# One turn and one product a pair in the first attention: VectorE combines both heads' weights

## The chip, the cores and the metric

The program runs on one core of one Trainium2 chip. The metric is device time in microseconds (us) of one execution, the median of several. Five engines share a core's on-chip memory, and each works through its own list of instructions in order: TensorE (PE: matrix products and transposes), VectorE (DVE), ScalarE (ACT), GpSimd (POOL) and SyncE (SP, here the DMA queue). They meet through semaphores: an instruction waits until a counter has reached a value, and another instruction raises it.

## The reference

The program computes two small transformer stacks one after the other on 256 tokens of width 1024, in float32. The change touches the first attention of the first stack only, the differential attention, once in each of its 2 layers (DEPTH = 2, A_HEADS = 4):

```python
y_a = diff_attention(aq.reshape(b, s, A_HEADS, 2, HEAD_DIM),
                     ak.reshape(b, s, A_HEADS, 2, HEAD_DIM),
                     av.reshape(b, s, A_HEADS, 2 * HEAD_DIM),
                     lam, lam_init, a_subln[i]).reshape(b, s, A_WIDTH)
```

Each of its 4 heads is a pair: two sets of queries and keys of width 64 give two score matrices of 256 by 256 with a mask by chunks of 64. Each has its own softmax, and both are applied to the same values of width 128. The output is the first product minus lambda times the second. Since the values are shared, (P1 V) - lambda (P2 V) is the same as (P1 - lambda P2) V, up to rounding.

## The kernel before

Tokens lie on the 128 partitions, in two tiles (T = 2). Weights come from HBM in tiles of 512 rows by up to 512 columns (1 MB), into a ring of 4 raw buffers. ScalarE copies each raw tile to a rounded "high" part (`high_part`, L1248), VectorE subtracts to get the "low" part (`low_part`, L1665), and TensorE makes three products for each of 4 row blocks and 2 token tiles (L665 to L667), 24 for a tile. High and low parts have 3 buffers, so that they are made some tiles ahead (`ahead`, which calls `split_to`).

The order of the work is written out by hand, in one program for each engine; no planner changes it later. A stage is a function of the same name on each engine. The stage here is `pairs` with `use == "A"`. `plan_of` deals out a list of weight tiles (the projections that later stages need) so that TensorE has products while a softmax goes on: one tile before and one after the first turn, then for pairs 0 to 3 the shares of 1, 2, 1 and 2 tiles, and two tiles held for the end (`hold`). The first two tiles in the shares have 324 columns, the others 512. Beside the tiles, the table `beside` gives VectorE work for the third attention (its norms and rotations: L1905, L1910, L1916 and the index keys, L1688 to L1979), which it does at a fixed place in its order.

For a pair n the chain is as follows, with a number of pairs of 4 in each of the 2 layers, so 8 in all.

- TensorE turns queries and keys (`start_turn_qk`, L763), ScalarE copies them (`copy_qk`, L1394), TensorE makes the scores of both heads into banks 5 and 6 (`pair_scores`, L779).
- VectorE adds the mask and takes the row maximum (`mid`, L2103 to L2112), ScalarE takes the exponential and the row sum (L1429), and VectorE takes the reciprocal of the sums and multiplies the second head's by minus lambda (`take_probs`, L2120 and L2123).
- TensorE turns the unscaled weights of both heads, 6 blocks (`turn_probs`, L818), ScalarE copies them in one piece of 768 columns (L1435), TensorE multiplies both with the values into bank 7 (`values`, L832).
- VectorE reads bank 7, scales the two halves by their row factors and adds them (`finish`, L2140 and L2143).

TensorE's place for this is fixed: scores of the pair, the tiles of its share up to three quarters of the last, the turn of the weights, the turn of the next queries and keys, the last quarter, and the products with the values. Where a share has one tile, that tile comes whole before the turn. VectorE's place is: mask and maximum of pair n, `finish` of pair n-1, the low parts of the share's tiles, the reciprocal, the work beside the tiles. ScalarE makes the high parts ahead of the exponentials.

After pair 3 TensorE starts on the two held tiles, and half way through the first it turns the index keys, which VectorE has to have rotated by then (`index_roped`). The next stage is `sticks` (the second attention), which ScalarE enters when VectorE has done its last instruction of `pairs` (`dve_done`).

## Time and profile before

| | us |
|---|---|
| median of 3 executions | 3175.24 |
| lowest, highest | 3172.05, 3179.62 |
| the profiled execution, its own time | 3178.99 |
| its span | 3177.2 |
| TensorE busy in the span | 3043.9 (96%) |
| VectorE busy | 2293.4 (72%) |
| ScalarE busy | 1755.9 (55%) |

The span is what the profiler saw from the first to the last instruction, and the device time of the same execution is 1.8 us longer. The two stages that the change touches run at about 77 to 142 us and 588 to 653 us of the span. TensorE's busy time counts a product until the modelled end of its result, so successive products overlap; how long one takes of the engine's time is read from the distance of two starts.

### The profile page before, as it was taken

What the parts mean: (1) busy time and instruction counts of PE and PEld (TensorE: products, weight loads), DVE (VectorE), ACT (ScalarE), POOL (GpSimd) and SP (SyncE); (2) the same over time, 40 slices, a digit from 0 to 9 for tenths busy, and PEclk for the clock granted to TensorE, in tenths of its full rate; (3) what the DMA queues carried; (4) which work ended last, traced back from release to release, by engine and by line L of the source; (5) the groups of instructions that cost most, each with busy time, mean ns of one, the idle gap of its engine ahead of it and who ended that gap; (6) DMA issues with size and microseconds to landing.
All of it is one profiled execution on the core that took longest, in us unless ns stands there. A gap on an engine that the chain in (4) does not pass through costs nothing.

```text
span 3177.2 us, 37793 instructions
## 1 busy us (share of the span) xinstructions
PE 3043.9 (96%) x14818; PEld 2484.5 (78%) x14818; DVE 2293.4 (72%) x2365; ACT 1755.9 (55%) x1657; POOL 46.2 (1%) x28
## 2 busy tenths in 40 slices
PE   8999999999999899998998999979999999999998
PEld 6777887877888787777887877768878888888786
DVE  7887556887645655776446666767888888888888
ACT  4565445465445345463433454626777777777765
POOL 0000000100000000000000000000000000000000
PEclk9999999999999999999999999989999999999999
DMA  7434555434555554335554543339999999999997
GB/s 247 146 128 157 185 183 174 161 120 142 179 186 179 170 168 160 119 133 185 185 172 159 181 163 110 129 97 344 347 359 338 349 361 338 353 361 343 359 342 260
DMA packets 351088, 697.24 MB, mean 219 GB/s; under 512 B 12224, under 2 KB 17216, under 8 KB 350784
## 3 DMA queue, kind: packets, MB, share of 16 engines
q1 hardware_dynamic: 347024, 687.75, 63.0%
q10 hardware_dynamic: 3888, 7.07, 0.7%
q8 instruction: 119, 1.95, 0.2%
q14 instruction: 57, 0.47, 0.0%
HBM read 693.73 MB, written 1.05 MB: 219 GB/s over the span
## 4 chain that ended last, share of the span: by engine, by line
PE 73%; DVE 11%; DMA 5%; ACT 4%; DVEq 3%; issue 3%; PEld 0%; POOL 0%; ACTq 0%; PEldq 0%
PE banks L665 22%; PE banks L667 21%; PE banks L666 21%; DVE weights_low L1665 5%; DMA weights_raw<-in_moe_w_down_dram 3%; ACT weights_high L1248 3%; DMA weights_raw<-in_moe_w_up_dram 1%; PE banks L1159 1%; PE banks L702 1%; DMA weights_raw<-in_moe_w_gate_dram 1%; PE banks L779 1%; PE banks L763 1%; PE banks L788 1%; PE banks L1097 1%; PE banks L1208 1%
## 5 line engine op out<-in xcount | busy, mean ns | idle before, releaser
L1665 DVE TENSOR_TENSOR weights_low<-weights_raw,weights_high 128x2048 fp32r<-128x2048 f32 (+1 forms) x658 | 1489.8, 2269 | 511.1 <-ACT weights_high L1248 506.3
L1248 ACT ACTIVATE weights_high<-weights_raw 128x2048 fp32r<-128x2048 f32 (+1 forms) x658 | 1247.4, 1899 | 551.0 <-PE banks L667 432.6
L665 PE MATMUL banks<-weights_high,h_transposed_high 128*128 128x512 f32 x2784 | 1107.5, 398 | 20.9 <-DVE weights_low L1665 11.0
L667 PE MATMUL banks<-weights_high,h_transposed_low 128*128 128x512 f32 x2784 | 1084.7, 390 | 0.0
L666 PE MATMUL banks<-weights_low,h_transposed_high 128*128 128x512 f32 x2784 | 1083.8, 389 | 0.0
L665 PEld LDWEIGHTS banks<-weights_high,h_transposed_high 128*128 128x128 f32 x2784 | 526.1, 189 | 145.5 <-DVE weights_low L1665 16.2
L667 PEld LDWEIGHTS banks<-weights_high,h_transposed_low 128*128 128x128 f32 x2784 | 525.7, 189 | 110.5
L666 PEld LDWEIGHTS banks<-weights_low,h_transposed_high 128*128 128x128 f32 x2784 | 526.7, 189 | 101.7 <-issue 1.0
L665 PE MATMUL banks<-weights_high,y_transposed_high 128*128 128x512 f32 x1000 | 396.8, 397 | 6.5 <-DVE y_transposed_low L2525 2.4
L667 PE MATMUL banks<-weights_high,y_transposed_low 128*128 128x512 f32 x1000 | 390.0, 390 | 0.0
L666 PE MATMUL banks<-weights_low,y_transposed_high 128*128 128x512 f32 x1000 | 389.5, 390 | 0.0
L665 PEld LDWEIGHTS banks<-weights_high,y_transposed_high 128*128 128x128 f32 x1000 | 187.7, 188 | 53.2 <-issue 7.1
L667 PEld LDWEIGHTS banks<-weights_high,y_transposed_low 128*128 128x128 f32 x1000 | 187.7, 188 | 40.0
L666 PEld LDWEIGHTS banks<-weights_low,y_transposed_high 128*128 128x128 f32 x1000 | 187.9, 188 | 36.9
L2560 POOL TENSOR_TENSOR rsqrt<-mean_squares,minus_half 128x2 f32<-128x2 f32 (+3 forms) x23 | 45.8, 1993 | 3124.1 <-DVE mean_squares L1677 1564.7
L1394 ACT ACTIVATE qk_transposed<-banks 128x512 f32<-128x512 f32 x68 | 38.6, 568 | 68.7 <-PE banks L763 64.4
L1367 ACT ACTIVATE projected<-banks 128x512 f32<-128x512 f32 x34 | 20.3, 596 | 97.2 <-PE banks L667 97.2
L1571 ACT ACTIVATE y_transposed_high<-banks 128x1024 fp32r<-128x1024 f32 (+1 forms) x22 | 22.2, 1007 | 87.4 <-PE banks L1097 87.4
L1429 ACT ACTIVATE scratch<-scratch,minus_row_max 128x256 f32<-128x256 f32 (+1 forms) x128 | 56.7, 444 | 24.7 <-DVEq L2112 24.4
L1304 ACT ACTIVATE h_transposed_high<-banks 128x512 fp32r<-128x512 f32 x32 | 17.9, 596 | 94.0 <-PE banks L702 94.0
L2397 DVE TENSOR_TENSOR y_transposed_low<-banks,y_transposed_high 128x1024 fp32r<-128x1024 f32 (+1 forms) x22 | 26.4, 1200 | 58.9 <-ACT y_transposed_high L1571 58.9
L702 PE MATMUL banks<-constants,x_residual 128*128 128x128 f32 x160 | 26.3, 319 | 39.7 <-DVE x_residual L2346 33.0
(326 smaller groups left out, 2184.5 us busy)
## 6 DMA issues: line engine op xcount, KB each, us to landing
weights_raw<-in_w_in_dram SPq DMA_DIRECT2D x152, 1024.0 KB, 5.0
weights_raw<-in_moe_w_gate_dram SPq DMA_DIRECT2D x114, 1024.0 KB, 6.6
weights_raw<-in_moe_w_up_dram SPq DMA_DIRECT2D x112, 1024.0 KB, 6.3
weights_raw<-in_moe_w_down_dram SPq DMA_DIRECT2D x112, 1024.0 KB, 6.5
weights_raw<-in_w_up_dram SPq DMA_DIRECT2D x32, 1024.0 KB, 5.4
weights_raw<-in_w_down_dram SPq DMA_DIRECT2D x32, 1024.0 KB, 5.0
weights_raw<-in_ffn_w_gate_dram SPq DMA_DIRECT2D x10, 1024.0 KB, 5.1
weights_raw<-in_ffn_w_up_dram SPq DMA_DIRECT2D x10, 1024.0 KB, 5.1
```

What stands on the lines that cost most here:

```text
L665: nc.tensor.matmul(out_of[t], lhs(0, k, t), high[:, k], start=begin, stop=False)
L666: nc.tensor.matmul(out_of[t], lhs(0, k, t), low[:, k], start=False, stop=False)
L667: mm = nc.tensor.matmul(out_of[t], lhs(1, k, t), high[:, k], start=False, stop=end)
L702: tr = nc.tensor.transpose(PS[:, t["banks"][b], at:at + P], buf[t["src"]][:, i, t["cols"][k]:t["cols"][k] + P], ident)
L763: tr = nc.tensor.transpose(PS[:, bank, i * P:(i + 1) * P], x[:, t, col:col + P], ident)
L779: mm = nc.tensor.matmul(PS[:, bank + h, cols], z[rows, q * P:(q + 1) * P], zk[rows, S:S + keys], start=True, stop=True)
L788: mm = nc.tensor.matmul(PS[h * HD:(h + 1) * HD, 7, col + cols.start:col + cols.stop], PR[:, kt, v0[h]:v0[h] + HD], weights[:, h, at:at + c ...
L1248: nc.scalar.activation(tile_view(WH, h % SPLIT, tile), tile_view(raw, h % RAW, tile), ACT.Copy).then_inc(high_ready, 1)
L1394: nc.scalar.activation(QKT[:, (n - 1) % 2, 0:cols], PS[:, bank, 0:cols], ACT.Copy).then_inc(qk_copied, 1)
L1429: nc.scalar.activation(probs, probs, ACT.Exp, bias=NMX[:, i:i + 1], accum_out=SUM[:, i:i + 1])
L1665: v.tensor_tensor(tile_view(WL, h % SPLIT, tile), tile_view(raw, h % RAW, tile), tile_view(WH, h % SPLIT, tile).bitcast(F32), ALU.subtract ...
L2560: nc.gpsimd.tensor_tensor(RSTD[:, 0:n], STAT[:, 0:n], MHALF[:, 0:n], ALU.pow).then_inc(rsqrt_ready, 1)
```

## The change

The second head's weights are scaled by its factor, the first head's are scaled and the second's added to them, by four VectorE instructions on the weights themselves, in place (`take_probs`). TensorE then turns 3 blocks and not 6 (`turn_combined`, into bank 7, whereas before they went to banks 5 and 6), ScalarE copies 384 columns and not 768, TensorE makes 3 products with the values and not 6 (`values_combined`, into bank 4), and `finish` is one copy.

The order changes on three engines. TensorE: the turn of the weights moves from three quarters of the last tile to its end, the next pair's scores come ahead of the products with the values, the share's last tile is always cut in quarters, and the turn of the next queries and keys, which writes the same bank 4, waits for `values_read`. ScalarE: the exponentials come ahead of the share's high parts, and the copy of queries and keys ahead of the copy of the turned weights. VectorE: `take_probs` always comes ahead of the share's low parts.

```diff
-                def turn_probs():
-                    pe.wait_ge(probs_ready, c.add("probs") + c.of("scaled"))
-                    for h in range(2):
-                        for i in range(3):
-                            tr = nc.tensor.transpose(PS[:, 5 + h, i * P:(i + 1) * P], SM[:, h, i * P:(i + 1) * P], ident)
+                def turn_combined():
+
+                    pe.wait_ge(probs_scaled, c.add("scaled"))
+                    wait_low(turned_in.get(7, 0))
+                    for i in range(3):
+                        tr = nc.tensor.transpose(PS[:, 7, i * P:(i + 1) * P], SM[:, 0, i * P:(i + 1) * P], ident)
                     tr.then_inc(probs_turned, 1)
...
+                def values_combined(n):
+
+                    _, _, (v0, _), _ = pair_cols(use, n)
+                    pe.wait_ge(probs_act, c.of("scaled"))
+                    pe.wait_ge(qk_copied, c.of("qk"))
                     for t in range(T):
-                        for h in range(2):
-                            for kt in range(t + 1):
-                                o = (2 * t + h) * vw
-                                mm = nc.tensor.matmul(PS[:, 7, o:o + vw], PT[:, h, (kt + t) * P:(kt + t + 1) * P],
-                                                      PR[:, kt, v0[h]:v0[h] + vw], start=kt == 0, stop=kt == t)
+                        for kt in range(t + 1):
+                            mm = nc.tensor.matmul(PS[:, 4, t * P:(t + 1) * P], PT[:, 0, (kt + t) * P:(kt + t + 1) * P],
+                                                  PR[:, kt, v0:v0 + P], start=kt == 0, stop=kt == t)
                     mm.then_inc(values_full, 1)
+                    c.add("values")
...
                 def pair_turn(n):
 
+                    if c.of("values"):
+                        pe.wait_ge(values_read, c.of("values"))
                     start_turn_qk(*pair_cols(use, n)[:2], bank=4 if use == "A" else 6, same_keys=use == "W" and n % 2 == 1)
...
                 if use == "A":
+                    pair_scores(5).then_inc(scores_full, 1)
                     for n in range(N):
-                        pair_scores(5).then_inc(scores_full, 1)
-                        late = shares[n][-1] if len(shares[n]) > 1 else None
-                        for p, i in shares[n]:
-                            if (p, i) != late:
-                                step(st, p, i)
-                        if late:
-                            for part in range(3):
-                                tile_step(*late, part, 4)
-                        turn_probs()
+                        for p, i in shares[n][:-1]:
+                            step(st, p, i)
+                        for part in range(3):
+                            tile_step(*shares[n][-1], part, 4)
                         if n + 1 < N:
                             pair_turn(n + 1)
-                        if late:
-                            tile_step(*late, 3, 4)
-                        values(n)
+                        tile_step(*shares[n][-1], 3, 4)
+                        turn_combined()
+                        if n + 1 < N:
+                            pair_scores(5).then_inc(scores_full, 1)
+                        values_combined(n)
...
                     act.drain().then_inc(probs_ready, 1)
                     if use == "A":
-                        act.wait_ge(probs_turned, c.add("turned_probs"))
-                        nc.scalar.activation(PT[:], PS[:, 5:7, 0:384], ACT.Copy).then_inc(probs_act, 1)
+                        for p, i in shares[n]:
+                            ahead(p, i)
+                            for what in beside_of(p, i):
+                                beside(p, what)
                         if n + 1 < N:
                             copy_qk(4)
+                        act.wait_ge(probs_turned, c.add("turned_probs"))
+                        nc.scalar.activation(PT[:, 0], PS[:, 7, 0:384], ACT.Copy).then_inc(probs_act, 1)
...
                         v.tensor_scalar(by_t(RS)[:, :, 1], by_t(RS)[:, :, 1], LAM[:, st["layer"], 1:2], None, ALU.mult)
                         dve.drain()
+                        one, two = (by_tile(SM[:, h]) for h in range(2))
+                        for t in range(T):
+                            v.tensor_scalar(two[t], two[t], RS[:, 2 * t + 1:2 * t + 2], None, ALU.mult)
+                        dve.drain()
+                        for t in range(T):
+                            i = v.scalar_tensor_tensor(out=one[t], in0=one[t], scalar=RS[:, 2 * t:2 * t + 1], in1=two[t],
+                                                       op0=ALU.mult, op1=ALU.add)
+                        i.then_inc(probs_scaled, 1)
...
-                        v.tensor_tensor(first, o[:, :, 0], by_t(RS)[:, :, 0].unsqueeze(2).broadcast_to([P, T, P]), ALU.mult)
-                        dve.drain()
-                        for t in range(T):
-                            i = v.scalar_tensor_tensor(out=PR[:, t, n * P:(n + 1) * P], in0=o[:, t, 1], scalar=RS[:, 2 * t + 1:2 * t + 2],
-                                                       in1=first[:, t], op0=ALU.mult, op1=ALU.add)
-                        i.then_inc(values_read, 1)
+                        v.tensor_copy(PR[:, :, n * P:(n + 1) * P], PS[:, 4, 0:S].rearrange("p (t d) -> p t d", t=T)).then_inc(values_read, 1)
...
+                    take_probs()
+                    for p, i in shares[n]:
+                        ahead(p, i)
```

The held tile's turn of the index keys also waits for `values_read` now, as it writes bank 4 too.

Two places show how the order moves. The first is TensorE around the last quarter of pair 1's second tile, before the change: L818 turns the weights (`scratch`), L763 turns the next queries and keys out of `projected`, L832 is the products with the values, L779 the scores.

```order
L818 MATMUL banks<-constants,scratch 128x128 [waits probs_ready]
L818 MATMUL banks<-constants,scratch 128x128 x5
L763 MATMUL banks<-constants,projected 128x128 [waits qk_copied]
L763 MATMUL banks<-constants,projected 128x128 x3
L665 MATMUL banks<-weights_high,h_transposed_high 128x512
L666 MATMUL banks<-weights_low,h_transposed_high 128x512
L667 MATMUL banks<-weights_high,h_transposed_low 128x512
L665 MATMUL banks<-weights_high,h_transposed_high 128x512
L666 MATMUL banks<-weights_low,h_transposed_high 128x512
L667 MATMUL banks<-weights_high,h_transposed_low 128x512
L832 MATMUL banks<-projected,weights_transposed 128x128 [waits values_read,probs_read_by_scalar]
L832 MATMUL banks<-projected,weights_transposed 128x128 x5
```

After the products with the values came the next scores (L779). The same place on TensorE in the changed kernel, where L762 is the turn of queries and keys, L664 to L666 are the tile's products, L818 is the turn of the combined weights and L778 the scores; the products with the values follow as L828, one and x2.

```order
L762 MATMUL banks<-constants,projected 128x128 [waits qk_copied,values_read]
L762 MATMUL banks<-constants,projected 128x128 x3
L664 MATMUL banks<-weights_high,h_transposed_high 128x512
L665 MATMUL banks<-weights_low,h_transposed_high 128x512
L666 MATMUL banks<-weights_high,h_transposed_low 128x512
L664 MATMUL banks<-weights_high,h_transposed_high 128x512
L665 MATMUL banks<-weights_low,h_transposed_high 128x512
L666 MATMUL banks<-weights_high,h_transposed_low 128x512
L818 MATMUL banks<-constants,scratch 128x128 [waits probs_scaled]
L818 MATMUL banks<-constants,scratch 128x128 x2
L778 MATMUL banks<-qk_transposed 128x128 [waits qk_copied]
L778 MATMUL banks<-qk_transposed 128x128
```

The turn of the weights moved behind the last quarter and halved, the scores moved ahead of the products with the values, and the wait for `values_read` moved from the products to the turn of queries and keys, which stands before the last quarter.

The second place is VectorE between the maximum of pair 1 and the start of pair 2, before the change: L2111 ends the maximum, L2140 and L2143 are `finish` of pair 0, L1665 the low parts of two tiles, L2120 and L2123 the reciprocal and lambda, L1910 and L1916 the norm beside the tiles, L2103 the mask and maximum of pair 2.

```order
L2111 TENSOR_SCALAR minus_row_max<-row_max 128x4
L2140 TENSOR_TENSOR scratch<-banks,row_scale 128x256 [waits values_full]
L2143 SCALAR_TENSOR_TENSOR projected<-banks,row_scale,scratch 128x128 x2
L1665 TENSOR_TENSOR weights_low<-weights_raw,weights_high 128x2048 [waits weights_high_ready] x2
L2120 RECIPROCAL row_scale<-row_sum 128x4 [waits probs_ready]
L2123 TENSOR_SCALAR row_scale<-row_scale,minus_lambda 128x2
L1910 TENSOR_TENSOR projected<-projected,rsqrt 128x2x1024 [waits rsqrt_ready]
L1916 TENSOR_TENSOR projected<-projected,parameters 128x512 x4
L2103 ISA scratch,row_max<-banks,constants 128x128 [waits scores_full]
```

The same place on VectorE in the changed kernel, with its own line numbers (L2142 is the copy that `finish` now is, L2123 and L2126 combine the weights, L1661 is the low parts, L1906 and L1912 the norm, L2099 the maximum of pair 2).

```order
L2107 TENSOR_SCALAR minus_row_max<-row_max 128x4
L2142 COPY projected<-banks 128x2x128 [waits values_full]
L2116 RECIPROCAL row_scale<-row_sum 128x4 [waits probs_ready]
L2119 TENSOR_SCALAR row_scale<-row_scale,minus_lambda 128x2
L2123 TENSOR_SCALAR scratch<-scratch,row_scale 128x128
L2123 TENSOR_SCALAR scratch<-scratch,row_scale 128x256
L2126 SCALAR_TENSOR_TENSOR scratch<-scratch,row_scale 128x128
L2126 SCALAR_TENSOR_TENSOR scratch<-scratch,row_scale 128x256
L1661 TENSOR_TENSOR weights_low<-weights_raw,weights_high 128x2048 [waits weights_high_ready] x2
L1906 TENSOR_TENSOR projected<-projected,rsqrt 128x2x1024 [waits rsqrt_ready]
L1912 TENSOR_TENSOR projected<-projected,parameters 128x512 x4
L2099 ISA scratch,row_max<-banks,constants 128x128 [waits scores_full]
```

The two low parts, which stood between the maximum and the wait for the exponentials, moved behind that wait, and four instructions came in.

## Rows read from the trace of the kernel before

**Rows 1.** The profile's page: the chain that ended last, by engine.

```profile
PE 73%; DVE 11%; DMA 5%; ACT 4%; DVEq 3%; issue 3%; PEld 0%; POOL 0%; ACTq 0%; PEldq 0%
```

**Rows 2.** Windows: stretch, length, busy PE, PEld, DVE, ACT, POOL; PEclk, DMA.

```profile
84.00:131.00 47.00, 46.07 (x273) 39.31 (x272) 38.59 (x94) 27.00 (x51) 6.12 (x2) 1.00 0.45 150
595.00:642.00 47.00, 46.08 (x274) 39.37 (x273) 38.63 (x94) 27.00 (x50) 6.12 (x2) 1.00 0.45 148
```

**Rows 3.** Timeline of PE: start, duration, engine, line, idle before.

```profile
83.23 0.93 PE L779 MATMUL banks<-qk_transposed 64*128 64x128 f32 x8
87.76 0.83 PE L818 MATMUL banks<-constants,scratch 128*128 128x128 f32 x6
88.43 0.60 PE L763 MATMUL banks<-constants,projected 128*128 128x128 f32 x4
89.49 1.60 PE L832 MATMUL banks<-projected,weights_transposed 128*128 128x128 f32 x12 [0.46 <-ACT weights_transposed L1435]
91.03 0.93 PE L779 MATMUL banks<-qk_transposed 64*128 64x128 f32 x8
...
114.12 0.50 PE L665 MATMUL banks<-weights_high,h_transposed_high 128*128 128x512 f32 x1
...
129.93 0.38 PE L763 MATMUL banks<-constants,projected 128*128 128x128 f32 x2
```

**Rows 4.** Waits of DVE from 84 to 131 us: us in total, times, longest.

```profile
DVE weights_low L1665 <- ACT weights_high L1248: 3.0, 2, 2.1
DVE scratch L2103 <- PE banks L779: 2.5, 2, 1.8
```

**Rows 5.** Timeline of DVE in pairs 0 to 3 of layer 0.

```profile
84.27 0.28 DVE L2103 CUSTOM_DVE_ANT_0 scratch<-banks,constants 128x128 f32<-128x128 f32 x1
85.86 2.29 DVE L1665 TENSOR_TENSOR weights_low<-weights_raw,weights_high 128x2048 fp32r<-128x2048 f32 x1
88.85 2.29 DVE L1905 TENSOR_REDUCE mean_squares<-scratch 128x32 f32<-128x2048 f32 x1
93.56 0.42 DVE L2140 TENSOR_TENSOR scratch<-banks,row_scale 128x256 f32<-128x256 f32 x1
94.59 2.28 DVE L1665 TENSOR_TENSOR weights_low<-weights_raw,weights_high 128x2048 fp32r<-128x2048 f32 x1
100.67 2.29 DVE L1910 TENSOR_TENSOR projected<-projected,rsqrt 128x2048 f32<-128x2048 f32 x1
105.46 0.28 DVE L2103 CUSTOM_DVE_ANT_0 scratch<-banks,constants 128x128 f32<-128x128 f32 x1
129.49 0.42 DVE L2140 TENSOR_TENSOR scratch<-banks,row_scale 128x256 f32<-128x256 f32 x1
```

**Rows 6.** Timeline of ACT in pair 0 of layer 0.

```profile
83.92 1.91 ACT L1248 ACTIVATE weights_high<-weights_raw 128x2048 fp32r<-128x2048 f32 x1
85.77 0.40 ACT L1429 ACTIVATE scratch<-scratch,minus_row_max 128x128 f32<-128x128 f32 x1
```

**Rows 7.** Timeline of ACT and DVE elsewhere: prices of what is new.

```profile
236.24 0.40 ACT L1429 ACTIVATE scratch<-scratch,minus_row_max 128x128 f32<-128x128 f32 x1 [3.74 <-DVEq L2112]
238.22 0.18 DVE L2120 RECIPROCAL row_scale<-row_sum 128x4 f32<-128x4 f32 x1 [2.05 <-ACTq L1432]
238.48 1.01 DVE L2129 TENSOR_SCALAR scratch<-scratch,row_scale 128x128 f32<-128x128 f32 x4
153.39 0.75 DVE L2044 SCALAR_TENSOR_TENSOR scratch<-scratch,projected,constants 128x128 f32<-128x128 f32 x2
```

**Rows 8.** Chain that ended last, in order of time, 119 to 165 us.

```profile
144.27 0.81 ACT scratch L1469
```

**Rows 9.** Timeline of PE in the stage after, and windows around its longest pause.

```profile
158.01 0.87 PE L788 MATMUL banks<-scratch,projected 128*64 128x256 f32 x8 [1.59 <-DVE scratch L2215]
214.02 1.71 PE L702 MATMUL banks<-constants,projected 128*128 128x128 f32 x8 [2.38 <-issue]
214.00:217.40 3.40, 3.38 (x13) 3.01 (x14) 2.80 (x7) 2.23 (x3) 0.00 (x0) 0.54 0.57 217
```

More of the change, by code:

```diff
@@ L359, in build @@
         IR = [b.rearrange("p (h k) -> p h k", h=2) for b in (S2f[:, 768:1536], S1f[:, 1024:1792])]
-        A1 = S1f[:, 768:1024].rearrange("p (t d) -> p t d", t=T)
         IDXM = S1f[:, 1536:1920]
@@ L901, in pairs @@
                             pair_scores(4, same_keys=use == "W" and n % 2 == 0).then_inc(scores_full, 1)
-                        pe.wait_ge(probs_act, c.of("probs") + c.of("scaled"))
+                        pe.wait_ge(probs_act, c.of("scaled"))
                         values_turned(st["given"], n, PT, pair_cols(use, n)[2], S)
@@ L907, in pairs @@
                 if use == "A":
-                    step(st, *hold[0], inside={2: lambda: (pe.wait_ge(index_roped, c.add("roped")), start_turn_qk(4608, 0, 4, keys=KI))})
+                    step(st, *hold[0], inside={2: lambda: (pe.wait_ge(index_roped, c.add("roped")), pe.wait_ge(values_read, c.of("values")), start_turn_qk(4608, 0, 4, keys=KI))})
                     index_scores(0)
@@ L1418, in pairs @@
                 for n in range(N):
-                    if use == "A":
-                        for p, i in shares[n]:
-                            ahead(p, i)
-                            for what in beside_of(p, i):
-                                beside(p, what)
                     act.wait_ge(max_ready, c.add("probs"))
@@ L2137, in finish @@
                         dve.wait_ge(values_full, c.add("values"))
-                        o = PS[:, 7, :].rearrange("p (t h d) -> p t h d", t=T, h=2)
-                        first = A1
-                        v.tensor_tensor(first, o[:, :, 0], by_t(RS)[:, :, 0].unsqueeze(2).broadcast_to([P, T, P]), ALU.mult)
-                        dve.drain()
-                        for t in range(T):
-                            i = v.scalar_tensor_tensor(out=PR[:, t, n * P:(n + 1) * P], in0=o[:, t, 1], scalar=RS[:, 2 * t + 1:2 * t + 2],
-                                                       in1=first[:, t], op0=ALU.mult, op1=ALU.add)
-                        i.then_inc(values_read, 1)
+                        v.tensor_copy(PR[:, :, n * P:(n + 1) * P], PS[:, 4, 0:S].rearrange("p (t d) -> p t d", t=T)).then_inc(values_read, 1)
                 before, after, shares, hold = plan_of(st)
@@ L2156, in pairs @@
                             take(p, i)
-                    if use == "A":
-                        late = n and any(p["use"] == "merge" and p["tiles"][i]["last"] for p, i in shares[n - 1])
-                        if not late:
-                            for p, i in shares[n]:
-                                ahead(p, i)
-                        take_probs()
-                        if late:
-                            for p, i in shares[n]:
-                                ahead(p, i)
-                    else:
-                        take_probs()
-                        for p, i in shares[n]:
-                            ahead(p, i)
+                    take_probs()
+                    for p, i in shares[n]:
+                        ahead(p, i)
                     for p, i in shares[n]:
```

7 lines of the change are left out of this document (removed).

## The prediction

> **What bounds the kernel now.** I read the page's chain of waits first. TensorE holds 73% of it and VectorE 11% [rows 1], so work taken from TensorE is gained in full wherever nothing else is late there, and nowhere else. Then the windows over the changed stretch, in both layers: TensorE busy 46.1 of 47 us, VectorE 38.6, ScalarE 27.0, clock 1.00, DMA share 0.45 [rows 2]. The two layers agree to 0.1 us, so I work out layer 0 and double it. TensorE seems the bound, but VectorE's waits in the same stretch are four, 5.5 us in all [rows 4]; the rest of its gaps is drains between instructions. VectorE is as good as full. The chain of waits by time says the same: at 144.27 us it goes through ScalarE's first instruction of the next stage (L1469) [rows 8], which starts when VectorE has ended its part of `pairs`. So two engines are close to the bound here, and each change is priced on both.
>
> **TensorE's side of the change.** Six turns take 0.67 us (87.76 to 88.43), three take about 0.33. The products with the values are 12 records (each float32 product shows as two) from 89.49 to 91.03, 1.54 us, and half of them 0.77 [rows 3]. That is 1.1 us less in each of 8 pairs, 8.8 us. The pairs with a share of one tile also wait for the copy of the turned weights, 0.46 us [rows 3], and the scores now stand in front of that wait (0.86 us of work): 4 such waits, 1.9 us. Were TensorE the only bound, 10.7 us would be gained.
>
> **VectorE's side.** New are two scalings and two multiply-adds for a pair. Four scalings of the same blocks take 1.01 us, so two 0.5; two multiply-adds of 128 and 256 columns out of on-chip memory take 0.75 [rows 7]; with a drain of 0.08 the combination costs 1.33 us, 5.3 us in the four pairs of a layer. `finish` was 1.03 us (93.56 to 94.59) [rows 5] and becomes one copy of 256 columns, for which I take the 0.42 of the read of 256 columns out of a bank (L2140) [rows 5] and 0.07 of drain, so 0.5: it gives back 0.53 a pair.
>
> The wait for the exponentials is the larger item. In the neighbouring attention the first exponential starts at 236.24 and the reciprocal at 238.22 after an idle 2.05 [rows 7], so 1.98 after it; the exponential starts 1.50 after the mask (84.27 to 85.77), so the reciprocal can come 3.48 after the mask's start, and VectorE is free of the mask after 1.59 (84.27 to 85.86) [rows 5, 6]. Before the change the low parts of the share, 2.3 us each, lay in this gap of 1.9 us. After it only `finish` of the last pair and the evacuation of a finished tile lie there, 0 in pair 0, then 0.5, 1.0 and 1.15. That leaves 1.9, 1.4, 0.95 and 0.75 idle, 5.0 us. Against it, the 5.5 us of VectorE's old waits [rows 4] go, since it will always be late for scores and high parts.
>
> VectorE's sum up to the rotated index keys: +5.0 (waits for exponentials) + 5.3 (combination) - 1.6 (`finish`, three times) - 5.5 (old waits) = +3.2 us. With the fourth `finish` it is +2.6 at its end of the stage.
>
> **Both sides on one clock.** I walk the pairs of layer 0, with 2.3 us for a low part and 1.9 for a high part [rows 5, 6], 0.23 for a product of 512 columns (42 products and nothing else lie between 114.12 [rows 3] and the next turn, 9.66 us), so 5.45 for a tile.
> - Pair 0. Mask at 84.27, reciprocal 87.75, plus 0.56 for it and lambda and 1.33: combined at 89.65. TensorE is through the 324-column tile and the next turn at 88.2 and waits 1.45 us. The high part is now behind the exponentials (87.7 to 89.6), then the copy of queries and keys, so that the scores start at 90.3 and the products with the values end at 91.9. That is where the next tile started before (91.9): pair 0 gains nothing.
> - Pair 1. VectorE: low part to 92.0, norm sums 2.5 (L1905 and its small follower) to 94.5, mask, reciprocal at 98.0, combined at 99.9. TensorE has two tiles to work on and does not wait. The next tile starts at 103.9, it was 104.4.
> - Pair 2. VectorE: two low parts to 104.5, then the norm, 4.8 us (100.67 to 105.46 [rows 5]), and the mask starts at 109.3 where it was 105.46. TensorE has done three quarters of its one tile at 108.0, and the next turn of queries and keys waits for `finish` of pair 1, at 111.4: 3.4 us idle. Then a quarter, and the combined weights come at 114.7: 1.4 us idle. The next tile starts at 116.9, it was 114.12 [rows 3].
> - Pair 3. Mask at 118.0, combined at 123.3, low parts to 127.9, index keys 4.65 to 132.6. TensorE's two tiles cover the softmax; the products with the values wait 0.75 for their copy, as no scores stand before them. TensorE reaches the turn of the index keys at 132.3 and gets it at 133.1, when `finish` is done; it was 129.93 [rows 3].
>
> So TensorE is 3.2 us late and VectorE 2.6. The stage after starts by VectorE's end (144.27) [rows 8], and its first pair has TensorE waiting 1.59 us for VectorE at 158.01 [rows 9]: there TensorE's extra 0.6 is absorbed and VectorE's 2.6 is passed on. I see nothing later that would swallow it: the weights are prefetched by four tiles, and DMA is at 0.45 [rows 2].
>
> Per layer +2.6 us, +5.2 in both. The profiled execution would be 3178.99 + 5.2 = 3184.2, and the median, 3.75 lower before, 3175.24 + 5.2 = **3180.4 us** (+0.16%). ScalarE: its exponentials are 8 by 1.9 us as before, the copy is shorter, and it has 20 us to spare in 47 [rows 2]. SP: low parts come up to 5.4 us later (96.9 against 102.2 in pair 1), so raw buffers are refilled later, against two tiles of slack; I cost that at nothing, and if the cover were gone, a late tile would cost a landing, several us.
>
> What the trace does not show is the copy out of a bank at 256 columns and the combination as a whole. Bounds: the copy 0.3 to 0.55, the combination 1.2 (no drain) to 1.8 (four instructions at 0.45 each, the multiply-add's upper half), so 4 x -0.5 to 4 x +0.5 for a layer, +0.6 to +4.6; I take 2.6 from the nearest rows. In both layers that is +1.2 to +9.2, 3176.4 to 3184.4.
>
> **The rivals.**
> - A, TensorE's saving counts: 10.7 us less, 3164.5. For it: TensorE is 98% busy in the stretch [rows 2]. Against: it needs VectorE to keep pace, and by the walk VectorE is 3.9 us behind at pair 2 already. If half of it is kept, 3170.
> - B, VectorE catches up and the two sides cancel, 3175. It needs the old waits of 5.5 us to be all that the change uses. Against: the sum has 10.3 us of new time a layer against 7.1.
> - C, slower by more: the pauses of pair 2 (3.4 and 1.4 us within 7) bring the clock down. The trace has a pause of 2.38 us at 214.02, and the granted clock of the next 3.4 us is 0.54, near the lower level of 1.2 GHz, against 1.00 around [rows 9]. At half the clock 3.4 us do 1.7 us of work. It costs nothing where TensorE waits anyway (1.4 us after the pause, 0.8 at the index keys, 0.6 in the next stage); it decides if it falls on the tiles of pair 3, with pauses long enough that it comes back. At its full price in both layers, +3.4: 3183.8, and with the combination at its upper bound 3188.
>
> The Trainium skill bears on C (TensorE: Matmul & The Clock Gate, "HAM oscillation"): pauses between bursts of products can bring the gate back to half rate, each time anew. The row at 214.02 agrees. By that rule alone the two layers would each lose the 1.7 us, by the walk's cover most of it disappears; my sum has it at zero.
>
> **How the numbers follow.** A median of this kernel tells no less than 0.2% (6.4 us) from no change. The forecast (3176.4 to 3184.4) has 0.52, A 0.08 in full and 0.07 for its half, B 0.10, C 0.23. Faster by over 0.2% is A, 0.13 with what of the half is under the bound. Slower by over 0.2% needs +6.4: all of C and 0.1 of the forecast's upper end, 0.33. Within: 0.54. The range from 3169 to 3188 leaves out A in full and the last of C.
>
> **What would show it.** In the profile after: TensorE idle 1 to 2 us before the turn of the combined weights in pairs 0 and 2, and some 3.4 us before the turn of queries and keys in pair 2, released by VectorE's copy; VectorE waiting for the exponentials before its reciprocal in all four pairs, 1.9 falling to 0.8; the four combining instructions in 1.3 us; the mask of pair 2 some 4 us later than 105.46; ScalarE's L1469 at 146.9 instead of 144.27. The forecast is wrong if VectorE has no wait before the reciprocal, if TensorE's pause in pair 2 is under 1 us, or if L1469 starts no later than before.

## The result, and the profile after

The change made the kernel slower by a quarter of a per cent: median 3185.40 us against 3179.84 us (18 executions each, side by side), ratio 1.0025 with a 95% interval of 1.0017 to 1.0033, which is 5.4 to 10.5 us, 8.0 in the middle (the two medians are 5.6 us apart, at the lower end of this). The forecast was +5.2 us. The ratios of the experiments below come from 6 to 12 executions of each kernel against 27 of the kernel before, and those intervals are wider.

The page of the kernel after: its span and the chain that ended last, by engine (before: [rows 1]).

```profile
span 3189.0 us, 37694 instructions
PE 76%; DVE 11%; ACT 4%; DMA 4%; DVEq 3%; issue 2%; PEld 0%; ACTq 0%; POOL 0%; PEldq 0%
```

The same stretch of both layers by windows, columns as in [rows 2].

```profile
84.00:131.00 47.00, 41.09 (x214) 32.95 (x212) 38.20 (x90) 23.38 (x49) 6.13 (x2) 0.93 0.39 131
599.20:646.20 47.00, 40.63 (x212) 32.76 (x210) 38.07 (x90) 23.24 (x49) 6.12 (x2) 0.93 0.39 131
```

TensorE's busy time in this window fell by 5.0 us (46.07 to 41.09), VectorE's stayed (38.59 to 38.20), and the mean granted clock went from 1.00 to 0.93. The 5.0 us are not all work saved: the stage is longer, so the same 47 us hold fewer products of the tiles. TensorE now stands idle between its pieces of work, as its timeline shows (layer 0; start, duration, idle before and who ended it). This layer starts 0.27 us later than before, and that is taken off wherever I compare.

```profile
90.03 0.55 PE L818 MATMUL banks<-constants,scratch 128*128 128x128 f32 x3 [1.40 <-DVE scratch L2126]
90.51 0.93 PE L778 MATMUL banks<-qk_transposed 64*128 64x128 f32 x8
102.62 0.93 PE L778 MATMUL banks<-qk_transposed 64*128 64x128 f32 x8 [0.45 <-ACT qk_transposed L1391]
111.54 0.66 PE L762 MATMUL banks<-constants,projected 128*128 128x128 f32 x4 [3.01 <-DVE projected L2142]
114.98 0.90 PE L818 MATMUL banks<-constants,scratch 128*128 128x128 f32 x3 [0.58 <-DVE scratch L2126]
115.81 1.66 PE L778 MATMUL banks<-qk_transposed 64*128 64x128 f32 x8
```

The scores (L778) take 0.93 us at 90.51 and 1.66 at 115.81: the clock has fallen in between. The windows give it.

```profile
84.00:111.80 27.80, 22.93 (x138) 19.07 (x137) 22.98 (x53) 12.71 (x30) 5.43 (x1) 1.00 0.41 141
111.80:118.60 6.80, 6.22 (x26) 4.25 (x25) 5.24 (x16) 4.54 (x9) 0.27 (x1) 0.55 0.05 8
```

In windows of 0.2 us the fall itself lies between 112.4 and 119.3 us; in layer 1 it is as long.

VectorE's waits in the stretch: those for the exponentials are as long as all its waits were before [rows 4], and 0.9 us for a high part come on top.

```profile
DVE row_scale L2116 <- ACTq L1424: 5.5, 4, 2.0
DVE weights_low L1661 <- ACT weights_high L1245: 0.9, 1, 0.9
```

The second of these waits is in pair 3, and comes from TensorE: ScalarE's high part there has waited 1.24 us for TensorE's products (timeline of ACT).

```profile
124.86 1.92 ACT L1245 ACTIVATE weights_high<-weights_raw 128x2048 fp32r<-128x2048 f32 x1 [1.24 <-PE banks L666]
```

VectorE's combination in pair 0:

```profile
88.03 0.18 DVE L2116 RECIPROCAL row_scale<-row_sum 128x4 f32<-128x4 f32 x1 [2.05 <-ACTq L1424]
88.59 0.55 DVE L2123 TENSOR_SCALAR scratch<-scratch,row_scale 128x128 f32<-128x128 f32 x2
89.22 0.75 DVE L2126 SCALAR_TENSOR_TENSOR scratch<-scratch,row_scale 128x128 f32<-128x128 f32 x2
90.00 2.29 DVE L1661 TENSOR_TENSOR weights_low<-weights_raw,weights_high 128x2048 fp32r<-128x2048 f32 x1
```

The stage's end is ScalarE's first instruction of the next attention (before: 144.27 [rows 8]), and the first wait of TensorE there (before: 158.01 [rows 9]), each 4.4 us later with the offset taken off.

```profile
148.94 0.81 ACT L1465 ACTIVATE scratch<-banks 128x768 f32<-128x768 f32 x1 [1.83 <-DVEq L2538]
```

```profile
162.68 0.87 PE L787 MATMUL banks<-scratch,projected 128*64 128x256 f32 x8 [1.59 <-DVE scratch L2202]
```

I call the time from TensorE's first scores of the layer to this ScalarE instruction the stage: 61.04 us before (83.23 to 144.27), 65.44 after (83.50 to 148.94); in layer 1 61.27 and 65.60. The two stages together are 8.7 us longer, and the measured ratio gives 8.0, so within the noise the loss is here. The profiled execution is a long one, 3190.80 us, and its span is 11.8 us longer than the one before; the 3.1 us outside the two stages are within what executions of one kernel differ by (3172 to 3186 us before). By "masks" I mean the starts of VectorE's mask and maximum in pairs 0 to 3, counted from the first: 0, 7.7, 21.2, 30.0 us before, 0, 10.3, 25.0, 33.6 after.

### The profile page after: what moved, and what is told of

It reads as the page before. It is cut to its first block, busy times and chain, and to the rows that moved or that the text cites. A ratio compares the mean times of both kernels' runs of the same rounds, so it can differ in the third digit from the quotient of the medians.

```text
span 3189.0 us, 37694 instructions
## 1 busy us (share of the span) xinstructions
PE 3048.3 (96%) x14746; PEld 2484.4 (78%) x14746; DVE 2300.0 (72%) x2381; ACT 1753.4 (55%) x1657; POOL 46.1 (1%) x28
## 4 chain that ended last, share of the span: by engine, by line
PE 76%; DVE 11%; ACT 4%; DMA 4%; DVEq 3%; issue 2%; PEld 0%; ACTq 0%; POOL 0%; PEldq 0%
PE banks L664 23%; PE banks L666 22%; PE banks L665 22%; DVE weights_low L1661 4%; ACT weights_high L1245 2%; DMA weights_raw<-in_moe_w_up_dram 1%; DMA weights_raw<-in_moe_w_down_dram 1%; PE banks L1156 1%; PE banks L701 1%; PE banks L762 1%; PE banks L787 1%; PE banks L778 1%; PE banks L1205 1%; PE banks L1094 1%; PE banks L841 1%
## 5 line engine op out<-in xcount | busy, mean ns | idle before, releaser
L1661 DVE TENSOR_TENSOR weights_low<-weights_raw,weights_high 128x2048 fp32r<-128x2048 f32 (+1 forms) x658 | 1490.1, 2269 | 507.5 <-ACT weights_high L1245 502.1
L664 PE MATMUL banks<-weights_high,h_transposed_high 128*128 128x512 f32 x2784 | 1110.6, 399 | 20.7 <-DVE weights_low L1661 10.5
L666 PE MATMUL banks<-weights_high,h_transposed_low 128*128 128x512 f32 x2784 | 1085.9, 390 | 0.0
L664 PEld LDWEIGHTS banks<-weights_high,h_transposed_high 128*128 128x128 f32 x2784 | 527.3, 189 | 145.7 <-DVE weights_low L1661 18.8
L666 PEld LDWEIGHTS banks<-weights_high,h_transposed_low 128*128 128x128 f32 x2784 | 526.6, 189 | 111.0
L664 PE MATMUL banks<-weights_high,y_transposed_high 128*128 128x512 f32 x1000 | 396.9, 397 | 4.2 <-DVE y_transposed_low L1778 1.5
L666 PE MATMUL banks<-weights_high,y_transposed_low 128*128 128x512 f32 x1000 | 390.4, 390 | 0.0
L664 PEld LDWEIGHTS banks<-weights_high,y_transposed_high 128*128 128x128 f32 x1000 | 188.1, 188 | 49.0 <-issue 6.2
L666 PEld LDWEIGHTS banks<-weights_high,y_transposed_low 128*128 128x128 f32 x1000 | 188.0, 188 | 40.1
L1364 ACT ACTIVATE projected<-banks 128x512 f32<-128x512 f32 x34 | 20.3, 597 | 99.5 <-PE banks L666 99.5
```

The costliest lines, as they stand in the source:

```text
L664: nc.tensor.matmul(out_of[t], lhs(0, k, t), high[:, k], start=begin, stop=False)
L666: mm = nc.tensor.matmul(out_of[t], lhs(1, k, t), high[:, k], start=False, stop=end)
L1661: v.tensor_tensor(tile_view(WL, h % SPLIT, tile), tile_view(raw, h % RAW, tile), tile_view(WH, h % SPLIT, tile).bitcast(F32), ALU.subtract ...
```

## The experiments

**The values in another bank.** After the change TensorE's longest pause (3.01 us) ends on the new wait for `values_read`. Here bank 4 isn't shared, so the wait isn't needed.

```diff
-                    pe.wait_ge(qk_copied, c.of("qk"))
...
-                            mm = nc.tensor.matmul(PS[:, 4, t * P:(t + 1) * P], PT[:, 0, ...
+                            mm = nc.tensor.matmul(PS[:, 7, t * P:(t + 1) * P], PT[:, 0, ...
...
-                    if c.of("values"):
-                        pe.wait_ge(values_read, c.of("values"))
...
-                        v.tensor_copy(PR[:, :, n * P:(n + 1) * P], PS[:, 4, 0:S]...
+                        v.tensor_copy(PR[:, :, n * P:(n + 1) * P], PS[:, 7, 0:S]...
```

The same wait goes from the turn of the index keys.

> The products with the values go to bank 7 (the turned weights there have been copied by then) and not to bank 4, so the next turn of queries and keys waits for no values_read; nothing else changes. I measure the stage in layer 0 from TensorE's first scores (L779 at 83.23 before) to ScalarE's first stick instruction (L1469 at 144.27 before): 61.0 us before, 65.4 after the change, of which I put 2.6 to VectorE's sum and 1.8 to the clock that fell to 0.55 for 6.8 us. Theory V (VectorE's order sets the stage's length, TensorE's pauses are only where it shows): the 3.0 us pause before the turn of queries and keys goes, and one pause of about 4.8 us before the turn of the combined weights takes its place (TensorE arrives near 109.9, combined weights at 114.7); the mask of pair 2 stays 25 us behind the first mask; the stage stays at 63.6 to 65.4, the kernel at +5 to +9 us against before. Rival B (the new wait on bank 4 is the cost): TensorE starts pair 3's tiles 3 us earlier, the stage is 60.6 to 62.4, the kernel within 3 us of before.

Measured: ratio 1.0036 (1.0023 to 1.0050), stage 65.85 and 65.73 us, third mask at 24.95. The one pause that is left in pair 2 (timeline of PE):

```profile
115.77 0.90 PE L818 MATMUL banks<-constants,scratch 128*128 128x128 f32 x3 [4.63 <-DVE scratch L2123]
```

The pause of 3.01 is gone and one of 4.63 stands at the next place where TensorE meets VectorE (I had put it at 4.8). Rival B falls: the bank's wait only shows VectorE's lateness. The stage is 0.3 to 0.5 us over what I had expected at most, and the kernel at +11.5 us by the ratio where I had +5 to +9: the clock fell for 6.8 us in both layers again, and 5.1 to 5.3 us of that lie behind the start of the turn of the combined weights, with no further pause in pair 2 to hide them (4.3 and 4.7 after the change).

**No combination.** Work left out, order kept.

```diff
-                        one, two = (by_tile(SM[:, h]) for h in range(2))
-                        for t in range(T):
-                            v.tensor_scalar(two[t], two[t], RS[:, 2 * t + 1:2 * t + 2], None, ALU.mult)
-                        dve.drain()
-                        for t in range(T):
-                            i = v.scalar_tensor_tensor(out=one[t], ...
-                        i.then_inc(probs_scaled, 1)
+                        dve.drain().then_inc(probs_scaled, 1)
```

> Leaves out the four instructions that scale and add the two heads' weights (the first head's unscaled weights are turned in their place); order and waits are those of the change. Theory V: 1.33 us a pair goes from VectorE, 5.3 a layer, so the mask of pair 2 comes 22.4 us after that of pair 0 (25.0 after the change, 21.2 before), TensorE's pause before the turn of queries and keys falls from 3.0 to 0.7 us, the clock stays up, the stage is 58.4 us and the kernel 5 us under before. Rival C (the clock and the wait on the bank make the loss, VectorE's new instructions are hidden): the pause and the stage are as after the change, 65.4, the kernel at +8.

Measured: ratio 1.0018 (1.0007 to 1.0028), stage 64.02 us, and the masks at 0, 10.3, 25.0, 33.6: not one of them moved. Theory V as I had put it is wrong here, and rival C is right that the new instructions are hidden. VectorE's waits say why (us, times, longest):

```profile
DVE weights_low L1661 <- ACT weights_high L1245: 6.0, 4, 1.5
DVE row_scale L2116 <- ACTq L1424: 5.5, 4, 2.0
```

Four new waits of 1.50 us for a high part stand where the combination was. ScalarE starts the high part (1.9 us) only when the exponentials are through, just when VectorE gets its sums, so the combination of 1.4 us lay beside a wait that the new order makes anyway. The pause of 3.01 us in pair 2 stayed too. But the clock did not follow it as in the first profile: it stayed at 1.00 through layer 0, and was down for 3.4 us in layer 1 (windows of the two stages):

```profile
84.00:150.00 66.00, 58.89 (x326) 46.65 (x325) 50.56 (x101) 32.61 (x59) 6.12 (x2) 1.00 0.43 147
604.00:665.00 61.00, 54.91 (x291) 43.51 (x291) 47.54 (x90) 30.31 (x51) 6.12 (x2) 0.97 0.41 138
```

That, and not the missing combination, is why the stage is 1.4 us shorter than after the change: with the clock up the changed kernel's stage is 64.06 (below).

**The old place of high and low parts**, with the combination, and then without.

```diff
-                    take_probs()
-                    for p, i in shares[n]:
-                        ahead(p, i)
+                    if use == "A":
+                        for p, i in shares[n]:
+                            ahead(p, i)
+                        take_probs()
...
+                    if use == "A":
+                        for p, i in shares[n]:
+                            ahead(p, i)
+                            for what in beside_of(p, i):
+                                beside(p, what)
                     act.wait_ge(max_ready, c.add("probs"))
...
-                        for p, i in shares[n]:
-                            ahead(p, i)
-                            for what in beside_of(p, i):
-                                beside(p, what)
```

> The change with the old place of the weight tiles' parts: ScalarE makes the share's high parts ahead of the exponentials, VectorE the low parts ahead of the reciprocal, in all pairs. Theory V: VectorE's waits for exponentials (5.5 us a layer after the change) shrink to about 0.3 in pairs 0 and 2, as low parts of 2.3 us lie in the gap of 1.9, but ScalarE's exponentials come behind high parts that wait for TensorE in pairs 1 and 3 (97.5 and 122.8, as before), so that little is won: mask of pair 2 22.4 us after the first, one pause of 3.2 us before the turn of pair 2's weights, stage 62.8 us without a fall of the clock and up to 64.6 with one, the kernel at +2 to +7 us. Rival R (the reordering alone makes the loss): all of it goes, stage 61.0 or less, the kernel at or under before.

Measured: ratio 1.0022 (1.0008 to 1.0036), stage 64.25 and 64.07 us, masks at 0, 8.4, 22.8, 31.1, TensorE's waits for the combined weights four:

```profile
PE banks L818 <- DVE scratch L2127: 6.1, 4, 2.8
```

The masks came as expected (22.4 expected for the third), the stage 1.3 to 1.5 us longer than the 62.8 I had walked: VectorE waits 3.5 us for the high part in pair 3, and TensorE waits in all four pairs where I had it wait in one. The clock stayed at 1.00. Rival R falls: undoing the reordering gives nothing back.

> The old place of high and low parts and, beside that, the four combining instructions left out (first head's unscaled weights turned). With the new place, leaving them out moved no mask (0, 10.3, 25.0, 33.6 us with and without), as VectorE then waited 1.50 us for the high part instead. Theory S (the combination costs only where no high part behind the exponentials covers it): here high parts come ahead, so it costs in full: masks at 0, 7.1, 19.8 and 26.6 us against 8.4, 22.8 and 31.1 with it, TensorE's waits before the turned weights 0.6, 0, 1.2, 0 against 1.9, 0.5, 2.8, 1.0, stage 58.2 us against 64.2. Rival (the combination is covered in this order too, and something else in the change makes the 64.2): stage over 62.5.

Measured: ratio 0.9997 (0.9987 to 1.0006), stage 59.01 and 59.31 us, masks at 0, 7.1, 20.3, 27.1 (0, 7.5, 20.6, 27.4 in layer 1). TensorE's waits for the turned weights:

```profile
PE banks L818 <- DVEq L2122: 1.8, 2, 1.3
```

In this order the four instructions cost 5.0 us a layer of the 5.6 that they take (four times 1.41, from 88.59 to 90.00 above). Theory S holds, with a stage 0.8 to 1.1 us over the 58.2 expected. The two switches together, stage in us, from layers whose clock stayed at 1.00 (the mean of both layers; 64.02 is layer 0 alone, as the clock fell in layer 1):

| | parts behind the exponentials (the change) | parts ahead of them (as before) |
|---|---|---|
| with the combination | 64.06 (the filled kernel below) | 64.16 |
| without | 64.02 | 59.16 |

So either the combination or the new order costs some 5 us, and the second of them comes free. Against the kernel before (61.15, which has the fuller work of TensorE and of `finish`) both together lose 2.9.

**The changed kernel again**, for the clock.

> The changed kernel again, for a second profile. In its first one the granted clock was 0.5 for 6.8 us in pair 2 of either layer; the same program's times run from 3182 to 3194 us. If the clock falls by chance, from one execution to the next, this profile can show a layer without it: stage 63.6 to 64.0 us there (VectorE's part alone) against 65.4 with it, the masks at 0, 10.3, 25.0 and 33.6 us in both cases. If the fall belongs to the pause itself, both layers show it again.

Measured: stage 64.02 us in layer 0 with the clock down for 3.4 us, 64.50 in layer 1 with 6.8 us; masks as before to 0.01. So the fall came again in both layers, but its length and its price differ (1.4, 1.5, about 0 and 0.4 us over 64.06 in four layers). It doesn't belong to the pause for certain either: the run without the combination had the same pause in layer 0 and no fall.

**The pause filled** with work of no use.

```diff
+                        if n == 2:
+                            for i in range(24):
+                                nc.tensor.transpose(PS[:, 7, 0:P], ident, ident)
                         if n + 1 < N:
                             pair_turn(n + 1)
```

> The change plus 24 turns of the identity into bank 7, which is free there, in front of the turn of queries and keys in pair 2: 2.7 us of work of no use inside the 3.0 us pause. Theory V with the clock as second part: the granted clock stays 1.00 through the stage in both layers, the masks stay at 0, 10.3, 25.0 and 33.6, the stage is 63.6 to 64.0 us instead of 65.4 and the kernel 3 us faster than the change. Rival: the fall of the clock costs nothing, as TensorE waits there anyway: the stage stays at 65.4, or grows by what the turns take over the pause.

Measured: stage 64.07 and 64.06 us, ratio 1.0019 (1.0010 to 1.0028) against 1.0025 for the change. The windows of this kernel around pair 2 and after it:

```profile
112.00:119.00 7.00, 5.25 (x32) 3.97 (x33) 5.44 (x13) 5.14 (x12) 0.00 (x0) 1.00 0.00 1
119.00:150.00 31.00, 29.98 (x152) 23.41 (x152) 27.12 (x54) 15.72 (x22) 0.70 (x1) 1.00 0.50 170
```

The clock stays at 1.00 and the stage is 1.4 to 1.5 us shorter than in the first profile, though TensorE does more. VectorE's wait of 0.9 us for the high part in pair 3 is gone too, as TensorE is no longer late there: by this wait the fall had reached VectorE. This separates the parts of the loss: 2.9 us a layer by VectorE (64.06 against 61.15), and 0 to 1.5 by the clock. In the whole kernel I had expected 3 us; the two ratios differ by 1.9 and their intervals overlap, so the second part is shown by the stages, not by the times. That the filler kept the clock up rests on two layers of one execution, and one layer with an unfilled pause had it up as well.

**The gap filled.** VectorE's first piece of work beside the tiles goes between `finish` and the reciprocal, where it waited for the exponentials.

```diff
+                    extra = [(p, what) for p, i in shares[n] for what in beside_of(p, i)]
+                    early = 1 if use == "A" else 0
+                    for p, what in extra[:early]:
+                        beside(p, what)
                     take_probs()
                     for p, i in shares[n]:
                         ahead(p, i)
-                    for p, i in shares[n]:
-                        for what in beside_of(p, i):
-                            beside(p, what)
+                    for p, what in extra[early:]:
+                        beside(p, what)
```

> The change with one more move: VectorE does the first piece of its work beside the tiles (norm sums, norm scale, index squares, index scale in pairs 0 to 3) between the end of the last pair's finish and the reciprocal, where it waited for the exponentials. Same instructions, same number. Theory V: the waits for exponentials (2.0, 1.7, 1.0 and 0.8 us after the change) go nearly all, the mask of pair 2 comes 21.8 us after the first (25.0), TensorE's pauses in pair 2 are 0.2 and 1.5 us, so the clock stays up; VectorE ends the stage 2.3 us earlier than before the change: stage 58.7 us, kernel 4 to 5 us under before. Rival B or C (bank wait, clock): the pause stays over 2.5 us and the kernel at +5 to +8. Rival E (TensorE bound by its own order, combined weights later in pairs 0 and 1 as the piece delays them): TensorE waits 2.1 us in pair 0 and the stage is 61 to 62.

Measured: stage 60.19 and 59.90 us, ratio 0.9994 (0.9985 to 1.0003), masks at 0, 8.3, 21.4, 29.3. VectorE's waits in the stretch in layer 0 (5.5 + 0.9 us after the change; in layer 1 one wait of 1.9 us for a high part is left), and TensorE's:

```profile
DVE scratch L2123 <- issue: 0.3, 1, 0.3
DVE mean_squares L1901 <- issue: 0.2, 1, 0.2
```

```profile
PE banks L818 <- DVE scratch L2126: 3.3, 2, 2.1
PE banks L828 <- ACT weights_transposed L1433: 0.6, 1, 0.6
```

The loss is gone with the same instructions in another order: VectorE's waits were the loss, and with them the pause of pair 2 went, and the fall of the clock. Against the kernel before no gain is shown, as the interval holds 1; I had expected 4 to 5 us. The stage is 1.5 us above the 58.7 of theory V, since TensorE's own waits bound it by then (2.1 and 1.2 for the combined weights, 0.6 for their copy), as rival E had it, though less than rival E's 61.

**The last turn earlier**, on top of that.

```diff
-                        tile_step(*shares[n][-1], 3, 4)
+                        if n + 1 < N:
+                            tile_step(*shares[n][-1], 3, 4)
                         turn_combined()
+                        if n + 1 == N:
+                            tile_step(*shares[n][-1], 3, 4)
```

> The kernel with VectorE's gap filled, and one more move: in pair 3 the combined weights are turned ahead of the last quarter of the last tile, so that the copy by ScalarE (a wait of 0.58 us before the products with the values) lies beside that quarter. VectorE has them combined 5 us earlier there. Expected: that wait is gone, TensorE's later work 0.6 us earlier, stage 59.4 us against 60.2 and 59.9, the kernel 1 us under the gap kernel, 2 to 4 us under before; no other wait changes. If the stage's end is set by VectorE, it stays at 60.0.

Measured: stage 59.60 and 59.55 us, median 3175.41 us (11 executions) against 3180.16 of before (27), ratio 0.9985 (0.9976 to 0.9994). TensorE's waits:

```profile
PE banks L818 <- DVE scratch L2129: 2.2, 1, 2.2
```

The 0.58 is gone, and this version is faster than the kernel before by 0.15%, and than the change by 0.4% if their two ratios are set against each other. The stages account for 3.2 us of its 4.8 against before. The wait of pair 2 (1.2 us) went too, which I had not expected. Its windows have the reason: the clock fell after the pause of pair 0, TensorE's scores of pair 2 came 1.6 us later than in the gap kernel (20.9 against 19.3 us from the first), and it then came to the combined weights too late to wait.

```profile
84.00:91.00 7.00, 4.84 (x33) 4.31 (x31) 6.35 (x19) 4.33 (x11) 2.45 (x1) 1.00 0.27 101
91.20:94.40 3.20, 3.20 (x17) 2.55 (x18) 3.00 (x11) 0.71 (x2) 2.78 (x1) 0.55 0.14 28
```

So the pause of 2.2 us in pair 0 is the longest that this version has left. No run tried to close it, and the wait in pair 2 may come back if the clock stays up. Nor did a run move the norm work or the last turn in the kernel before, so it is open how much of the 0.15% belongs to combining the weights.

## Why the prediction was right, and where it was short

- **The numbers.** +8.0 us lies in the forecast's +1.2 to +9.2, but nearer to rival C's +8.6 than to its own +5.2. The prediction gave 0.54 to a change within 0.2% and 0.33 to slower by more; it became slower by 0.25%, on the less likely side. The lower bound, 4 x -0.5, also doesn't follow from its terms: 1.2 in place of 1.33 and 0.3 in place of 0.5 give -0.3 a pair.
- **TensorE's side.** 1.1 us less a pair was foreseen; in pair 0 the three turns take 0.48 (with the start after a wait) where six took 0.67, and the products with the values 0.69 where they took 1.54, so 1.04 less. In the change it brought nothing, since TensorE waited for VectorE: right. With the old order and nothing in its place on VectorE, it and the shorter `finish` together are worth 2.0 us a layer (61.15 to 59.16).
- **VectorE's sum.** The waits for exponentials are 5.5 us (5.0 forecast), the combination 1.4 us a pair (1.33). The sum gave +2.6 us a layer, and the kernel with the clock up measures +2.9: right in size. The old waits of 5.5 us went, as forecast; of the two profiles of the change only the first has the 0.9 us for a high part, and the filled kernel, with the clock up, hasn't.
- **The combination as a term** was read wrongly. I booked 5.3 us to it. Leaving it out moved no mask, for the high part behind the exponentials makes VectorE wait 1.50 us at that place. I had the high part's new place in the walk (87.7 to 89.6, combined at 89.65) and did not see that the two ends fell together. The whole came out right because in the new order the one costs what the other would have cost (the table above), which the sum doesn't say: in part luck. Who had followed the sum and made the combination cheaper would have gained nothing at the masks.
- **The walk.** With 0.27 taken off: combined weights turned at 89.76 (forecast 89.7), third mask 109.23 (109.3), turn of queries and keys 111.27 after 3.01 idle (111.4 after 3.4), fourth mask 117.89 (118.0). Up to there each step stands within 0.4 us. In the filled kernel, counted from the first scores, the walk holds to its end: `finish` of pair 3 starts at 132.43 (the walk has the index keys done at 132.6), L1469's counterpart at 147.3 (146.9). A wait of 0.45 us in pair 1, before the scores, was not in it.
- **The clock** is where it was short. "My sum has it at zero" failed in part: the fall came in both layers, for 6.8 us and not 3.4, and reached past the 1.4 us of idle that was to hide it, onto the scores, the products with the values and the first products of pair 3, which starts at 118.43 and not 116.9. The second pause, put at 1.4 us, shrank to 0.58, as the last quarter of the tile ran slower. That is 1.4 and 1.5 us a layer in the first profile, and 0 and 0.4 in the second, so the zero of the sum is near the truth in some executions and not in others. The level was as the row at 214.02 had shown [rows 9]. The Trainium skill (TensorE: Matmul & The Clock Gate, "HAM oscillation") says that pauses between bursts can bring the gate back to half rate, each time anew. Both layers of the first profile agree, at 0.55; the run without the combination, whose layer 0 stayed at 1.00 after the same 3.01 us of idle, does not agree with "each time".
- **The passing on.** The next attention took the lateness in full: TensorE's first wait there is 1.59 us again, 4.4 us later. Right.
- **The rivals.** A and B did not come about. C did in mechanism, with 0 to 1.5 us a layer in place of 1.7, on top of 2.9 and not of 2.6.

## What to carry to other kernels

Where two engines are both nearly full, work moved from one to the other has to be priced at the receiver's waits, and the order of the receiver's list decides more than the instructions: here the same change loses 0.25%, or nothing that can be told from noise, by where some norm work stands on VectorE, and with one of TensorE's turns moved as well it gains 0.15%. Before booking a cost, ask what the engine would wait for if the instruction were not there. An engine that waits for another's result should find work without that dependency in front of the wait.

## What the runs showed of the hardware

- The same pause brought different falls of the granted clock to its 1.2 GHz level. After 3.0 us of idle it was down for 6.8 us in three layers, for 3.4 us in two and not at all in one (the change twice, and the kernel without the combination). After 4.6 us, with the values in another bank, it was down for 6.8 us in both layers. Pauses of 2.16 and 2.14 us were followed by a fall of 3.4 us in both layers of the last version, while pauses of 2.13 and 2.11 us (gap kernel) and of 2.78 and 2.63 us (old place of the parts) were not.
- Of the nine falls in these stages five began with TensorE at work again (0.8 to 1.7 us after it had started), and four while it still stood idle (the two with the values in another bank, and one layer each of the second profile and of the kernel without the combination).
- The price of a fall on the changed kernel's stage lay between nothing and 1.5 us, by what wait it ran into. In the last version it made TensorE's scores of pair 2 come 1.6 us later, and took a wait of 1.2 us away.
- 24 turns of the identity (2.79 us) inside such a pause, and the clock stayed at 2.4 GHz in both layers; two layers are too few to say that it always would.
